# State-space scan: the block between the two chunks as one product per four heads

## What is computed

```python
def step(state, inp):                       # one chunk of 128 tokens
    xc, dtc, bc, cc = inp
    cum = jnp.cumsum(dtc * A, axis=1)
    seg = cum[:, :, None] - cum[:, None, :]
    decay = jnp.exp(jnp.where(causal, seg, -jnp.inf))
    cb = jnp.einsum('btgn,bsgn->btsg', cc, bc)
    w = cb[..., None] * decay * dtc[:, None]
    y = jnp.einsum('btsgk,bsgkp->btgkp', w, xc)
    y = y + jnp.einsum('btgn,bgkpn->btgkp', cc, state) * jnp.exp(cum)[..., None]
    w_end = jnp.exp(cum[:, -1:] - cum) * dtc
    state = (state * jnp.exp(cum[:, -1])[..., None, None]
             + jnp.einsum('bsgk,bsgkp,bsgn->bgkpn', w_end, xc, bc))
    return state, y
```

## Time and profile before

| | |
|---|---|
| three runs | 1258.87, 1258.96, 1260.46 us; median 1258.96 |
| span of the profiled execution | 1257.2 us from the first to the last instruction |
| TensorE busy | 1242.1 us, 99% |
| VectorE busy | 932.5 us, 74% |
| ScalarE busy | 684.2 us, 54% |
| the scan | from about 666 to 780 us of the span |

### The profile page before, as it was taken

The page is one execution under the profiler, slowest core; times in us unless marked ns, Lnnn a source line. Parts: engine busy times, 40 slices in busy tenths (PEclk is TensorE's granted clock), DMA queues, the critical chain, the costliest instruction groups (busy, mean ns, idle before and its releaser), DMA issues. The chain is left out here.

```text
span 1257.2 us, 18334 instructions
## 1 busy us (share of the span) xinstructions
PE 1242.1 (99%) x7514; PEld 1102.9 (88%) x7514; DVE 932.5 (74%) x1292; ACT 684.2 (54%) x872; POOL 68.2 (5%) x93
## 2 busy tenths in 40 slices
PE   9999999999999999999999999999999999999997
PEld 8878999989988888889998888888888888888886
DVE  6676857875456666577997998788888868788877
ACT  6654444343553444455777655466655574566652
POOL 2000000100000000000003331000000000000000
PEclk9999999999999999999999999999999999999999
DMA  9664545656435665647656654655554744655551
GB/s 294 219 184 144 185 143 188 214 186 209 168 101 170 199 194 178 197 138 219 185 168 210 203 191 151 217 185 201 184 186 138 231 134 134 201 194 179 197 194 41
DMA packets 162595, 227.97 MB, mean 181 GB/s; under 512 B 7853, under 2 KB 123825, under 8 KB 162384
## 3 DMA queue, kind: packets, MB, share of 16 engines
q1 hardware_dynamic: 159392, 216.68, 53.5%
q0 software_dynamic: 2816, 9.52, 2.3%
q10 hardware_dynamic: 304, 0.59, 0.1%
HBM read 225.68 MB, written 1.10 MB: 180 GB/s over the span
## 5 line engine op out<-in xcount | busy, mean ns | idle before, releaser
L1310 DVE TENSOR_TENSOR wlo<-raw,whi 128x2048 fp32r<-128x2048 f32 (+3 forms) x185 | 415.9, 2260 | 113.9 <-ACT whi L830 112.8
L830 ACT ACTIVATE whi<-raw 128x2048 fp32r<-128x2048 f32 (+3 forms) x185 | 345.9, 1883 | 16.0 <-DMA raw<-in_w_xkv 6.1
L2159 PE MATMUL psum<-h_both,whi 128*128 128x512 f32 x714 | 254.7, 396 | 0.0
L2158 PE MATMUL psum<-h_both,wlo 128*128 128x256 f32 x714 | 199.4, 279 | 0.3 <-DVE h_both L1364 0.3
L2125 PE MATMUL psum<-h_both,whi 128*128 128x256 f32 x688 | 195.9, 285 | 0.0
L2127 PE MATMUL psum<-h_both,wlo 128*128 128x256 f32 x688 | 194.6, 283 | 0.0
L2126 PE MATMUL psum<-h_both,whi 128*128 128x256 f32 x688 | 194.6, 283 | 0.0
L2125 PE MATMUL psum<-whi,r_hi 128*128 128x512 f32 x446 | 176.6, 396 | 0.0
L2127 PE MATMUL psum<-whi,r_lo 128*128 128x512 f32 x446 | 173.9, 390 | 0.0
L2126 PE MATMUL psum<-wlo,r_hi 128*128 128x512 f32 x446 | 173.8, 390 | 0.0
L2159 PEld LDWEIGHTS psum<-h_both,whi 128*128 128x128 f32 x714 | 134.0, 188 | 27.6
(11 more groups left out here) (350 smaller groups left out, 1807.1 us busy)
## 6 DMA issues: line engine op xcount, KB each, us to landing
raw<-in_ffn_up SPq DMA_DIRECT2D x40, 1024.0 KB, 5.1
raw<-in_w_in SPq DMA_DIRECT2D x31, 1024.0 KB, 5.8
raw<-in_ssd_in_proj SPq DMA_DIRECT2D x22, 1024.0 KB, 5.4
raw<-in_ffn_down SPq DMA_DIRECT2D x22, 1024.0 KB, 4.9
raw<-in_w_up SPq DMA_DIRECT2D x16, 1024.0 KB, 5.6
raw<-in_w_down SPq DMA_DIRECT2D x16, 1024.0 KB, 4.9
raw<-in_w_xkv SPq DMA_DIRECT2D x8, 1024.0 KB, 5.2
raw<-in_ssd_out_proj SPq DMA_DIRECT2D x8, 1024.0 KB, 5.2
```

The source lines that it names most:

```text
L830: A(whi[u % SLOTS][:, 0:kt * n], raw[u % SLOTS][:, 0:kt * n], ACT.Copy).then_inc(hi_split, 1)
L1310: V.tensor_tensor(wlo[s][:, 0:kt * n], raw[s][:, 0:kt * n], whi[s][:, 0:kt * n].bitcast(F32), ALU.subtract).then_inc(lo_split, 1)
L2158: M(b[:, 0:T], w_lo_k, h_hi[:, k, :], start=False, stop=False)
L2159: return M(b[:, :], w_hi_k, h_both[:, :, k, :], start=False, stop=k == kt - 1)
```

## The change

The middle block (chunk 0 by chunk 1) is taken out of the tiles of the single heads. Its decay is exp(cum at t) times exp(sum from s to the end of chunk 0), so it splits into a factor by row and a factor by column. The inputs of chunk 0, times the second factor and dt, form `x_end` (256 columns for the four heads of a group); one product of the group's scores (copied by ACT to SBUF, `cbT`) with `x_end` gives the whole block for four heads; DVE multiplies the result by the first factor (`since`) in its PSUM bank (`scale_off`); and the heads' two remaining products add to that.

- A third product of 32 columns (`after`, the strict upper triangle) joins the cumulative sums; ACT makes both factors from them (`to_end`, `since`) behind its table load.
- For groups 0 and 1, `x_end` is made from x * dt and `to_end`; from group 2 on from the raw x and `to_end_dt`, at head 8q + 5, for the two groups from 8q + 8 on.
- The ring's tiles and the decay rows have 256 columns in place of 384, `crow` is one instruction in place of three, and four rows in place of three are asked for first. The scores of group 0 are made two steps earlier.

```diff
@@ -91,7 +91,9 @@
     what, h = SSD_STEPS[n + 1] if n + 1 < len(SSD_STEPS) else ("none", 0)
-    return h // 4 if what == "head" and h % 4 == 0 else None
+    if n == 1:
+        return 0
+    return h // 4 if what == "head" and h and h % 4 == 0 else None
...
-        dec = [dec0[:, :]] + [rows[:, 1, TRI * b:TRI * b + TRI] for b in range(2)] + [room(14336 + TRI * b, TRI) for b in range(3)]
+        dec = [rows[:, 1, T * b:T * b + T] for b in range(4)] + [room(14336 + T * b, T) for b in range(2)]
+        after = dec0[:, 0:P]
+        x_end = [dec0[:, 0:T], room(14848, T)]
+        cbT = [dec0[:, T:TRI], room(15104, P)]
+        to_end, since = negcum[:, 0, 1, :], negcum[:, 1, 1, :]
+        to_end_dt = dtb[:, 0, :]
...
-                elif h == 3:
+                elif h == 4:
                     wait_bank(sp, ("xsN", 7))
...
-            rows_at = {at[("zz", 0, 0)] + SLOTS - 1: [0, 1, 2], at[("zz", 0, 1)] + SLOTS: [3, 4, 5]}
+            rows_at = {at[("zz", 0, 0)] + SLOTS - 1: [0, 1, 2, 3], at[("zz", 0, 1)] + SLOTS: [4, 5]}
...
+            wait_drained(act, "cum")
+            A(to_end, to_end, ACT.Exp).then_inc(factors_ready, 1)
+            A(since, negcum[:, 1, 0, :], ACT.Exp, scale=-1.0).then_inc(factors_ready, 1)
+
+            def copy_scores(g):
+                b = wait_bank(act, ("CB", g))
+                if g >= 2:
+                    act.wait_ge(off_done, g - 1)
+                A(cbT[g % 2], b[:, P:T], ACT.Copy).then_inc(cb_copied, 1)
...
-                A(d[:, 0:T], d[:, 0:T], ACT.Exp, bias=negcum[:, 0, 0, h:h + 1])
-                A(d[:, T:TRI], d[:, T:TRI], ACT.Exp, bias=negcum[:, 1, 0, h:h + 1]).then_inc(s_exp, 1)
+                A(d[:, 0:P], d[:, 0:P], ACT.Exp, bias=negcum[:, 0, 0, h:h + 1])
+                A(d[:, P:T], d[:, P:T], ACT.Exp, bias=negcum[:, 1, 0, h:h + 1]).then_inc(s_exp, 1)
...
                     if (u, n) == (0, 3):
+                        copy_scores(0)
                         decay(0)
...
                     if what == "head":
+                        if h and h % 4 == 0:
+                            copy_scores(h // 4)
...
+            def scale_to_end(g, factor):
+
+                if g < 2:
+                    dve.wait_ge(xdt_ready, 2)
+                    dve.wait_ge(factors_ready, 2)
+                else:
+                    wait_drained(dve, ("xsN", g))
+                    dve.wait_ge(off_done, g - 1)
+                if g == 1:
+                    wait_bank(dve, ("xsN", 7))
+                heads = slice(4 * g, 4 * g + 4)
+                V.tensor_tensor(x_end[g % 2].rearrange("p (h d) -> p h d", d=SSD_P),
+                                xsN[:, 0, 256 * g:256 * g + 256].rearrange("p (h d) -> p h d", d=SSD_P),
+                                factor[:, heads].unsqueeze(2).to_broadcast([P, 4, SSD_P]), ALU.mult).then_inc(x_end_ready, 1)
+
+            def scale_off(g):
+
+                dve.wait_ge(off_done, g + 1)
+                y = bank[use[("y", g)][0]][:, T:2 * T].rearrange("p (h d) -> p h d", d=SSD_P)
+                V.tensor_tensor(y, y, since[:, 4 * g:4 * g + 4].unsqueeze(2).to_broadcast([P, 4, SSD_P]), ALU.mult).then_inc(off_scaled, 1)
...
             prepare(0)
+            scale_to_end(0, to_end)
...
-                        V.tensor_tensor(dec[h % SSD_RING], dec[h % SSD_RING], b[:, 0:TRI], ALU.mult)\
+                        if h % 4 == 0:
+                            dve.wait_ge(cb_copied, h // 4 + 1)
+                        d = dec[h % SSD_RING].rearrange("p (a t) -> p a t", a=2)
+                        V.tensor_tensor(d, d, b[:, 0:2 * T].rearrange("p (a t) -> p a t", a=2)[:, :, 0:P], ALU.mult)\
                             .then_inc(done(("CB", h // 4)) if h % 4 == 3 else s_w, 1)
+                        if h % 4 == 1:
+                            scale_off(h // 4)
+                        if h == 1:
+                            scale_to_end(1, to_end)
+                            chain(V.tensor_tensor(to_end_dt, to_end, dtv[:, 0, :], ALU.mult))
+                        if h % 8 == 5 and q < 3:
+                            for g in (2 * q + 2, 2 * q + 3):
+                                scale_to_end(g, to_end_dt)
...
+            def ssd_off(g):
+
+                pe.wait_ge(cb_copied, g + 1)
+                pe.wait_ge(x_end_ready, g + 1)
+                y_next[:] = [claim(("y", g))]
+                M(y_next[0][:, T:2 * T], cbT[g % 2], x_end[g % 2], start=True, stop=True).then_inc(off_done, 1)
...
                 if h % 4 == 0:
-                    y_bank[:] = [claim(("y", h // 4))]
+                    y_bank[:] = y_next
+                    pe.wait_ge(off_scaled, h // 4 + 1)
...
-                M(y_0, s[:, 0:P], xsN[:, 0, xs], start=True, stop=True)
-                M(y_1, s[:, P:T], xsN[:, 0, xs], start=True, stop=False)
-                M(y_1, s[:, T:TRI], xsN[:, 1, xs], start=False, stop=True).then_inc(ssd_y, 1)
+                M(y_0, s[:, 0:P], xsN[:, 0, xs], start=False, stop=True, skip_group_check=True)
+                M(y_1, s[:, P:T], xsN[:, 1, xs], start=False, stop=True, skip_group_check=True).then_inc(ssd_y, 1)
...
                     if h >= 2:
                         ssd_y_of(h - 2)
+                    if h % 4 == 0:
+                        ssd_off(h // 4)
```

More of the change, by code:

```diff
@@ L518, in build @@
         expa = sb("expa", [P, SSD_HEADS])
-        crow = sb("crow", [SSD_HEADS, TRI])
+        crow = sb("crow", [SSD_HEADS, T])
         dec0 = sb("dec0", [P, TRI])
-        decay_rows = nc.dram_tensor("decay_rows", (SSD_HEADS, TRI), F32, kind="Internal").ap()
+        decay_rows = nc.dram_tensor("decay_rows", (SSD_HEADS, T), F32, kind="Internal").ap()
         ARENA = 15500
@@ L620, in build @@
         low_out = sem("low_out")
-        dt_sum, dt_log, dta_ready, cum_row = sem("dt_sum"), sem("dt_log"), sem("dta_ready"), sem("cum_row")
+        dt_sum, dt_log, dta_ready = sem("dt_sum"), sem("dt_log"), sem("dta_ready")
+        factors_ready, cb_copied, x_end_ready, off_done, off_scaled = (
+            sem(n) for n in ("factors_ready", "cb_copied", "x_end_ready", "off_done", "off_scaled"))
         s_conv, s_silu, xdt_ready, s_w, ssd_y, y_done = (sem(n) for n in ("s_conv", "s_silu", "xdt_ready", "s_w", "ssd_y", "y_done"))
@@ L780, in _ @@
             after_norm(3)
-            pool.wait_ge(cum_row, 1)
+            wait_drained(pool, "cumT")
             pool.dma_start(decay_rows[:, :], crow[:, :]).then_inc(rows_stored, 16)
@@ L785, in _ @@
                 d = dec[h % SSD_RING]
-                diagonal = d.rearrange("p (a t) -> p a t", a=3)[:, 0:3:2, :]
+                diagonal = d.rearrange("p (a t) -> p a t", a=2)
                 nc.gpsimd.tensor_tensor(diagonal, diagonal, big2, ALU.add).then_inc(row_masked, 1)
@@ L1829, in _ @@
                     sums = b[:, 0:2 * SSD_HEADS].rearrange("p (t h) -> p t h", t=NT)
-                    V.tensor_scalar(negcum[:, :, :, :], sums.unsqueeze(2).to_broadcast([P, NT, 2, SSD_HEADS]), -1.0, None, ALU.mult)\
-                        .then_inc(done("cum"), 1)
+                    V.tensor_copy(to_end, b[:, 2 * SSD_HEADS:3 * SSD_HEADS])
+                    V.tensor_scalar(negcum[:, :, 0, :], sums, -1.0, None, ALU.mult).then_inc(done("cum"), 1)
                 if m == 7:
                     b = wait_bank(dve, "cumT")
[L1834 to L1839, removed]
+                    V.tensor_scalar(crow[:, :], b[0:SSD_HEADS, 0:T], -1.0, None, ALU.mult).then_inc(done("cumT"), 1)
                 wait_drained(dve, key)
@@ L1851, in _ @@
                 if m == 0:
+                    V.tensor_scalar(after, tri, -1.0, 1.0, ALU.mult, ALU.add).then_inc(dta_ready, 1)
                     dve.wait_ge(dt_log, 2)
@@ L2682, in _ @@
                 if m == 4:
-                    pe.wait_ge(dta_ready, 2)
+                    pe.wait_ge(dta_ready, 3)
                     pe.wait_ge(cst_in, 16)
@@ L2687, in _ @@
                     for t in range(NT):
-                        last = M(b[:, SSD_HEADS * t:SSD_HEADS * (t + 1)], tri, dta[:, t, :], start=True, stop=True)
+                        M(b[:, SSD_HEADS * t:SSD_HEADS * (t + 1)], tri, dta[:, t, :], start=True, stop=True)
+                    last = M(b[:, 2 * SSD_HEADS:3 * SSD_HEADS], after, dta[:, 0, :], start=True, stop=True)
                     last.then_inc(fill("cum"), 1)
@@ L2693, in _ @@
                     for t in range(NT):
-                        last = nc.tensor.transpose(b[0:2 * SSD_HEADS, P * t:P * t + P], negcum[:, t, :, :].rearrange("p a h -> p (a h)"), ident)
+                        last = nc.tensor.transpose(b[0:SSD_HEADS, P * t:P * t + P], negcum[:, t, 0, :], ident)
                     last.then_inc(fill("cumT"), 1)
@@ L2708, in _ @@
             xs_transpose(6)
-            y_bank, so_banks = [], []
+            y_bank, y_next, so_banks = [], [], []
             def ssd_scores(g):
```

## The result

The changed kernel takes 1261.47 us (median of 16 runs, 1260.70 to 1264.52) against 1258.96 (16 runs): ratio 1.0021, 95% interval 1.0014 to 1.0028. It is slower by 0.2%, or 2.5 us; in the two profiled executions the span goes from 1257.2 to 1259.2 us. That lies within the range of the forecast, 1256.8 to 1263.2, and above its 1260.2: the change costs twice the 1.25 us of the sum. The mechanism that it named is there: PE has less work and waits more. The likeliest outcome by its chances was no measurable change (0.57); a slower kernel had 0.32.

The account below looks back on a forecast made before the run. PE, busy 99% of the span, was taken as the bound, with new waits in its queue deciding; +2.2 +1.1 -0.6 -0.55 +0 -1.1 +0.2 made +1.25 us on 1258.96, so 1260.2 us, range 1256.8 to 1263.2.

Parts of the forecast that it names:

- PE's work, -3.3 us: On PE, 7.2 us of per-head products go; eight off products add 3.7, the 32-column product for the sums 0.2.
- +0.2 ahead of the scan: Before the scan, the added 32-column product for the sums makes PE about 0.2 us later.
- DVE's prices: On DVE, a product takes 0.41 us; each `scale_off` or `scale_to_end` 0.41, or 0.34 in a queue.
- The start: PE waits 1.75 us at off(0) for ACT's copy, 1.0 at y(0) for `scale_off`; lateness +3.2, then +2.2 at y(2).
- Group 2: At y(8), PE waits 1.5 us for `scale_off(2)`, against none before; lateness against before +3.3 us.
- Round 2: No wait at y(16); the rest of PE's saving becomes waiting at yT, so the round gives only -0.55 us.
- Round 3 and after: PE waits 1.2 us at y(24) for `scale_off(6)`, round gives 0; five heads after the last yT give -1.1.
- Behind the scan everything hangs on PE and moves along.: After the scan, everything follows PE, so its lateness carries through with no further term in the sum.
- DVE becomes the bound all through: Rival: from 0.2 us more per `scale_to_end` and `scale_off`, DVE decides through the scan; +1.8 us more, 1262.0; 24%.
- The clock: Rival: waits at off(0) and y(0) drop PE to 1.2 GHz, up to 2.4 us more to y(2), 1262; 5%.
- PE's saving arrives whole: Rival: DVE and ACT run far enough ahead that no new wait is left; -3.3 us, 1255.7; 12%.
- The copy is not last: Rival: off never waits, start included, only y for `scale_off`; y(0) still waits for product(1); 1259.8; 8%.

Follow-up runs that it names:

- e1: Changed kernel with `scale_off` of the even groups placed on DVE right behind product(4g), ahead of the next half weight split and product(4g+1): 1258.60 us.
- e4: Changed kernel with the call of `scale_off` and PE's wait for it deleted: 1258.28 us.
- e2: Changed kernel with only the first block product, off(0), issued one head step later on PE: 1262.95 us.
- e3: Changed kernel with both edits, even groups' `scale_off` behind product(4g) and off(0) one head step later: 1257.56 us.
- e6: On top of e3, POOL's load of the next norm's bias row ahead of the last root; one execution, stretch behind the scan 14.59 us against 14.93.
- e8: On top of e3, DVE takes the group norm's statistics ahead of the half weight split, three times: 1256.61 us.
- e9: On top of e8, the next norm's bias row loaded earlier and ACT's first copy of the scores ahead of its half weight split: 1256.47 us.
- e5: On top of e3, each group's scaled inputs made in its own head step from x*dt, not three heads ahead from raw inputs: 1270.88 us.
- e7: On top of e3, middle block left out: no off products, `scale_off`, scaled inputs or copies of scores: 1255.78 us.
- e10: Kernel before the change with statistics ahead of the half weight split and the bias row's load ahead of the last root: 1258.10 us.

## Why the prediction was right, and where its steps were not

- **Waits, not work.** Right, and shown by e1 and e4: the places of four instructions are worth 2.9 us, and the removal of all eight 3.2, which cannot be told from that.
- **PE's work, -3.3 us.** Measured -3.0. The sum has a slip: 32 x 0.22 is 7.0, not 7.2, so its terms give -3.1. A head of y is 0.22 shorter. off was taken at 0.46: from y(2) through off(1) to y(3) PE takes 2.26 us, from y(3) to y(4) without one 1.84, so 0.42.
- **+0.2 ahead of the scan.** Wrong in sign: the last transposes in front of the scan start at 672.80 instead of 673.01, and the wait of 0.2 us that PE had for ACT in 600 to 673 us is gone. The added product did cost its 0.2 us where it stands (the transposes of `cumT` start at 617.35 instead of 617.14), but the next transposes, at 632.15 before, lost a wait of 0.24 and start at 631.95. Why that wait went is not shown; the step had put the product on the path without looking for the next wait.
- **DVE's prices.** Right: product 0.41, `scale_off` and `scale_to_end` 0.42. Only the 32-column scaling at head 1 took 0.72, off the path.
- **The start.** Right in its times: off(0) starts at 675.12 (forecast 675.1), y(0) at 679.51 (679.55), shift +3.19 for +3.2, and +2.16 for +2.2 at y(2). That the wait of 1.72 us fits 1.75 is in part luck: the forecast counts from start to start, and by that measure PE, which came 0.21 us earlier, waits 1.96 us at off(0), and 1.11, 1.34, 0.73 and 1.68 us at y(0), y(8), y(16) and y(24). The idle times that the rows show are some 0.15 to 0.24 us shorter. e2 and e3 show what the sum could not: the two waits are one budget.
- **Group 2.** The wait at y(8) was 1.34 instead of 1.5, shift +3.0 instead of +3.3. The term held within its stated 0.4.
- **Round 2.** This step failed: "no wait" at y(16), measured 0.57 in the row, 0.73 from start to start. The step priced prepare's multiplications as unchanged. prepare(2) took 3.84 us from its start to product(16) instead of 3.03 (713.78 to 716.81 before), so `scale_off(4)` ended at 721.63, not 0.1 us ahead of PE. The stretched pieces lie beside POOL's masks, for some 2.1 us now and 1.1 before; that these are the cause is argued, not shown. The rival of DVE as the bound had named such stretching, in round 2 among others; only its size was wrong. The effect on the sum was small, since PE's wait at yT(2), predicted with some 0.8, was paid at y(16) instead.
- **Round 3 and after.** The wait at y(24) was 1.68 instead of 1.2, outside the stated 0.4, so the round gave +0.30 instead of 0; then -0.98 to y(31) against -1.1 forecast. At y(31) the shift is +1.08; the steps give +1.05 there without the 0.2. That they meet so closely is luck: -0.26 in group 2 and +0.30 in round 3 cancel.
- **"Behind the scan everything hangs on PE and moves along."** Failed by 0.7 us, the largest miss. 0.36 of it is the stretch of e6, which hangs on the last weight pieces. Another 0.36 lies between the second and third transposes of the next norm: 5.82 or 5.83 us in the changed kernel, e1, e2, e3, e6, e8 and e9, 5.47 or 5.48 in the kernel before, e4, e5, e7 and e10. As e5 has `scale_off`, that is not the cause. It lies in the low part `h_both` on DVE (shown with the result), which starts 0.29 us behind the instruction ahead of it, and for which PE's next product waits; what held it the profile does not say, and it stays open. With these the span grew by 2.0 us rather than 1.25. The medians lie 2.5 us apart, since the profiled execution of the changed kernel took 1261.04 us, 0.43 below its median.
- **The rivals.** The time alone does not refute two of them: 1261.47 lies nearer to their 1262 than to the forecast's 1260.2. *DVE becomes the bound all through*: `scale_off` and `scale_to_end` took 0.42 us rather than 0.6, and e4 speaks against it. *The clock*: stays at 1.00 in the scan here, falls in e2 and e5. *PE's saving arrives whole*: the best version, e9, gains 2.4 us; e7, with 7.0 us of products gone, 3.2, as yT binds. *The copy is not last*: PE waited 1.72 us for it, and it ended at 675.02, 0.58 behind the inputs (674.44).
- **The bounds.** "1257.5 to 1262" does not follow from its parts: four waits good to 0.4 and 0.2 x 8 for off give 1258.6 to 1263.4. The result lies within both.

## What to carry to other kernels

When work is split so that a small step on another engine comes between two products, give that step a place ahead of the long instructions in its queue, not the place where its program text ended up: here four steps of 0.42 us cost 4.2 us of waits by standing behind a 1.2 us split each, and moving them gave 2.9 us back. Before counting a saving on the busiest engine, look for the next thing that it meets; here the waits at yT, and what lies behind the scan, kept over half of it (3.8 of 7.0 us) even with a free middle block. Two waits that hang on the same late engine are one budget, and removing the first alone can make a worse second.

## What the runs showed of the hardware

One long wait took the clock down where two shorter ones had not. Single waits of PE of 2.35, 2.53, 3.00 and 3.32 us were followed by the 1.2 GHz level while PE was fully busy again; waits of 1.72, 1.78, 1.86 and 1.88 us were not. The Trainium skill, "TensorE: Matmul & The Clock Gate", Part 1, says that the throttled state is the default and activity releases it: the rows agree, as PE worked two to four us at 0.50 to 0.59 and was then back at 1.00.

One place goes either way. Far behind the scan, two waits of 0.69 and 0.86 us stand 1.5 us apart in every kernel. In the profiled executions of the changed kernel, of e8 and of e2:

```profile
980.00:985.00 5.00, 3.45 (x21) 1.00 0.71 140
```

```profile
980.00:985.00 5.00, 4.99 (x22) 0.66 0.63 210
```

```profile
985.00:990.00 5.00, 4.13 (x18) 0.71 0.48 157
```

The same work, once at the full clock, twice not. The clock fell there in five of the profiled executions (e2, e4, e7, e8, e9), and these took 1.3 to 2.2 us more than the medians of their kernels; in those of the changed kernel, e1, e3, e5 and e10 it did not fall, and they took no more than theirs. So spans of two profiles should not be compared to better than such a fall: e8's of 1256.3 us is longer than e3's 1255.8, though its median is 1.0 shorter.
